# Down projection in a conv FFN: a third pair of output tiles by seven products, with Pool's weight sums held back

## The reference

```python
def conv_ffn(h, w_up, conv_w, conv_b, w_down):
    u = h @ w_up
    c = u.shape[-1]
    u = lax.conv_general_dilated(u, conv_w[:, None, :].astype(u.dtype), window_strides=(1,),
        padding=[(CONV_WIDTH - 1, 0)], dimension_numbers=("NWC", "WIO", "NWC"), feature_group_count=c) + conv_b
    a, gate = jnp.split(u, 2, axis=-1)
    return (jax.nn.silu(gate) * a) @ w_down

x = x + conv_ffn(h, ffn_w_up[layer], ffn_conv_w[layer], ffn_conv_b[layer], ffn_w_down[layer])
```

## Time and profile before

| what | value |
|---|---|
| median of three runs | 3196.84 us (3196.56 to 3198.14) |
| the profiled execution | 3196.49 us |
| its span, first to last instruction | 3194.6 us |
| mean granted TensorE clock | 0.999 |
| PE busy | 3179.1 us, 100% of the span |
| DVE busy | 2049.5 us, 64% |
| ACT busy | 1298.8 us, 41% |
| POOL busy | 503.0 us, 16% |

### The profile page before, as it was taken

One profiled execution on the slowest core, in us unless ns is written; L12 is line 12 of the kernel. 1 busy time (PEld: TensorE's weight loads), 2 busy tenths in 40 slices (PEclk: granted clock), 3 DMA queues, 4 the chain that ended last, 5 costly groups with the idle time before them and its releaser, 6 DMA issues.

```text
span 3194.6 us, 45570 instructions
## 1 busy us (share of the span) xinstructions
PE 3179.1 (100%) x16502; PEld 2681.1 (84%) x16502; DVE 2049.5 (64%) x2876; ACT 1298.8 (41%) x1758; POOL 503.0 (16%) x436
## 2 busy tenths in 40 slices
PE   9999999999999999999999999999999999999998
PEld 7788888889998788888889998768888888888887
DVE  8455567586557455567586555666877744588776
ACT  4433333334443433333334453354443523554433
POOL 2100000123221100000123221052202101322111
PEclk9999999999999999999999999999999999999999
DMA  7256324423333156324423332203233332122332
GB/s 268 67 167 208 125 93 167 142 93 106 100 105 101 58 165 205 130 92 164 146 91 108 99 102 87 86 21 101 97 106 99 105 99 92 47 79 93 105 99 79
DMA packets 100044, 359.31 MB, mean 112 GB/s; under 512 B 11057, under 2 KB 13361, under 8 KB 99761
## 3 DMA queue, kind: packets, MB, share of 16 engines
q1 hardware_dynamic: 98960, 354.08, 33.6%
q0 software_dynamic: 928, 3.17, 0.3%
HBM read 355.11 MB, written 2.10 MB: 112 GB/s over the span
## 4 chain that ended last, share of the span: by engine, by line
PE 94%; DVE 1%; POOLq 1%; issue 1%; ACT 1%; DMA 1%; DVEq 0%; SPq 0%; ACTq 0%; POOL 0%
PE pb L759 21%; PE pb L761 21%; PE pb L760 21%; PE pb L1074 6%; PE pb L1314 3%; PE pb L829 2%; PE pb L831 2%; PE pb L830 2%; PE pb L791 1%; PE pb L792 1%; PE pb L795 1%; PE pb L1182 1%; PE pb L1613 1%; DMA raw<-stream 1%; PE pb L1615 1%
## 5 line engine op out<-in xcount | busy, mean ns | idle before, releaser
L2348 DVE TENSOR_TENSOR lo<-raw,hi 128x1024 fp32r<-128x1024 f32 (+1 forms) x484 | 601.5, 1249 | 320.6 <-ACT hi L1685 294.8
L1685 ACT ACTIVATE hi<-raw 128x1024 fp32r<-128x1024 f32 x484 | 508.5, 1056 | 730.8 <-PE pb L761 436.3
L759 PE MATMUL pb<-yH,hi 128*128 128x512 f32 (+1 forms) x1664 | 644.7, 387 | 0.0
L760 PE MATMUL pb<-yL,hi 128*128 128x512 f32 (+1 forms) x1664 | 644.5, 387 | 0.0
L761 PE MATMUL pb<-yH,lo 128*128 128x512 f32 (+1 forms) x1664 | 644.4, 387 | 0.0
L759 PE MATMUL pb<-hH,hi 128*128 128x512 f32 x1128 | 440.8, 391 | 0.0
L760 PE MATMUL pb<-hL,hi 128*128 128x512 f32 x1128 | 439.3, 389 | 0.0
L761 PE MATMUL pb<-hH,lo 128*128 128x512 f32 x1128 | 439.2, 389 | 0.0
L761 PEld LDWEIGHTS pb<-yH,lo 128*128 128x128 f32 x1664 | 312.6, 188 | 63.7
L760 PEld LDWEIGHTS pb<-yL,hi 128*128 128x128 f32 x1664 | 312.6, 188 | 63.2
L759 PEld LDWEIGHTS pb<-yH,hi 128*128 128x128 f32 x1664 | 312.7, 188 | 63.0
(11 more groups left out here) (537 smaller groups left out, 5550.1 us busy)
## 6 DMA issues: line engine op xcount, KB each, us to landing
raw<-stream SPq DMA_DIRECT2D x648, 512.0 KB, 3.4
yF<-first SPq DMA_DIRECT2D x8, 512.0 KB, 11.9
act<-first SPq DMA_DIRECT2D x8, 512.0 KB, 16.5
x<-xT SPq DMA_DIRECT2D x4, 512.0 KB, 7.0
outT<-act SPq DMA_DIRECT2D x7, 256.0 KB, 2.2
act<-crow POOLq DMA_DIRECT2D x2, 512.0 KB, 5.4
tab<-decay SPq DMA_DIRECT2D x1, 1024.0 KB, 7.7
scr<-ws POOLq DMA_DIRECT2D x2, 256.0 KB, 3.1
```

What stands on the lines that cost most here:

```text
L759: pe.matmul(out, whi, ahi, start=first, stop=False)
L760: pe.matmul(out, whi, alo, start=False, stop=False)
L1685: act.activation(hi[:, s], raw[:, s], ACT.Copy).then_inc(hi_ready, 1)
L2348: dve.tensor_tensor(lo[:, s, 0:width], raw[:, s, 0:width], hi[:, s, 0:width].bitcast(F32), ALU.subtract).then_inc(lo_ready, 1)
```

## The change

Pair two (g = 1) is done by seven products as well, so that `fast_down` on PE keeps two plain tiles in place of four. Its four weight sums are rounded and subtracted one at a time, in the order in which PE wants them (first sum, e2, e4, e3). For all three fast pairs the first sum goes to a buffer of its own instead of over the raw tile; ACT and DVE split only the second half of the pair's second tile, and the first sum separately. PE takes the product with token sum four before the one with the first weight sum. Pool makes t1 of the last token part (DVE did); the fourth token sum's last part is rounded and split ahead of the second and third. Pool starts the weight sums when that fourth one is split (`m_lo` at 6 x slab + 5), where it used to start with `m_last`. SP's load of pair four's tiles now waits for pair two's weight sums, because `DOWN_GROUPS` holds g = 1.

The diff, cut to its core:

```diff
-FAST_DOWN, DOWN_GROUPS = (0, 1), (2, 3)
+FAST_DOWN, DOWN_GROUPS = (0, 1), (1, 2, 3)
...
+                pool.wait_ge(p_full, 5 * (at - 1 if g == 3 else at if g == 1 else at - 2))
+                pool.tensor_tensor(one, a21, a22, ALU.add)
+                pool.drain().then_inc(s1_ready, 1)
+                pool.tensor_tensor(e2, one, a11, ALU.subtract)
...
+                pool.tensor_tensor(e4, a12, e2, ALU.subtract)
...
+                pool.tensor_tensor(e3, a11, a21, ALU.subtract)
+                pool.drain().then_inc(w_sums, 1)
...
-                    pool.wait_ge(m_last, d_slab(layer, j) + 1)
+                    b1, t1 = d_even, d_raw(1, 3)
+                    pool.wait_ge(product, made + KT - 1)
+                    pool.tensor_tensor(t1, b1[:, TH[1]], b1[:, TH[0]], ALU.subtract)
+                    pool.drain().then_inc(m_first, 1)
+                    pool.wait_ge(m_lo, 6 * d_slab(layer, j) + 5)
                     for g in DOWN_GROUPS:
                         down_sums(layer, j, g)
...
-                for group in (range(3), (3,)):
-                    for m in range(KT):
...
+                for m in range(KT):
+                    w = slice((m % 2 * 4 + m // 2) * P, (m % 2 * 4 + m // 2 + 1) * P)
+                    pe.wait_ge(y_ready, y0 + m + 1)
+                    for s in range(2):
+                        ins = three(pb[:, s], hi[:, s, w], lo[:, s, w], midH[:, m], midL[:, m], m == 0, m == KT - 1)
...
-                product_of(other_sum, own(s1, 0), token(1)).then_inc(p_full, 1)
-                product_of(lower_sum, own(s1, 1), token(4)).then_inc(tile_done, 1)
-                pe.wait_ge(e_lo, at + 1)
+                product_of(lower_sum, own(s1, 1), token(4)).then_inc(p_full, 1)
+                pe.wait_ge(e_lo, e_count(layer, j, g) - (3 if g == 1 else 1))
+                product_of(other_sum, own(s1, 0), token(1)).then_inc(tile_done, 1)
+                if g == 1:
+                    pe.wait_ge(m_lo, tokens_made)
+                pe.wait_ge(e_lo, e_count(layer, j, g) - (2 if g == 1 else 0))
                 pe.wait_ge(x_part, added + 1)
                 product_of(one_sum, summed_w(2), token(2), False).then_inc(p_full, 1)
...
+                    if fast:
+                        down_hi(layer, j, 1, 1)
+                        act.wait_ge(m_first, slab + 1)
+                        middle_hi(3, 0, 1)
                     gate(n - 1)
...
                         act.wait_ge(m_last, slab + 1)
-                        middle_hi(3)
-                        tick(0)
+                        middle_hi(3, 3)
+                        middle_hi(3, 1, 3)
+                        down_sum_hi(layer, j, 1)
...
+                elif i == 0:
+                    dve.wait_ge(s1_ready, one_count(layer, j, g) + 2)
...
+                middle_lo(layer, j, 3, 3)
+                down_one_lo(layer, j, 1)
+                middle_lo(layer, j, 3, 1, 3)
+                plain_add(0)
+                one()
+                down_sum_lo(layer, j, 1, 0)
+                plain_add(1)
+                lower()
+                down_sum_lo(layer, j, 1, 2)
+                other()
+                two()
+                down_sum_lo(layer, j, 1, 1)
+                down_lo(layer, j, 2, 0)
+                upper()
+                down_lo(layer, j, 2, 1)
+                last()
                 one, other, two, lower, upper, last = x_adds(layer, j, 2)
+                down_one_lo(layer, j, 2)
+                one()
                 down_sum_lo(layer, j, 2)
-                one()
+                lower()
+                other()
+                two()
                 down_lo(layer, j, 3, 0)
-                other()
-                lower()
-                two()
+                upper()
                 down_lo(layer, j, 3, 1)
-                upper()
                 last()
...
+                    if fast:
+                        down_lo(layer, j, 1, 1)
+                        middle_lo(layer, j, 3, 0, 1)
                     multiplied(n - 1)
```

More of the change, by code:

```diff
@@ L310, in build @@
         d_product = lambda layer, j: layer * (sum(SLABS) - len(SLABS)) + sum(SLABS[:j]) - j
+        d_middle = lambda layer, j: 56 * LAYERS + 8 + layer * (sum(SLABS) + 12) + sum(SLABS[:j])
         gain2 = sb("gain2", [P, 8])
@@ L1281, in fast_down @@
             def fast_down(layer, j, y0):
-                for group in (range(3), (3,)):
-                    for m in range(KT):
[L1285 to L1293, removed]
+                for s in range(2):
+                    pe.wait_ge(lo_ready, tiles.next())
+                    pe.wait_ge(bank_free, banks.next())
+                for m in range(KT):
+                    w = slice((m % 2 * 4 + m // 2) * P, (m % 2 * 4 + m // 2 + 1) * P)
+                    pe.wait_ge(y_ready, y0 + m + 1)
+                    for s in range(2):
+                        ins = three(pb[:, s], hi[:, s, w], lo[:, s, w], midH[:, m], midL[:, m], m == 0, m == KT - 1)
+                        if m == KT - 1:
+                            ins.then_inc(tile_done, 1)
                 for g in DOWN_GROUPS:
@@ L1299, in down_group @@
                 q, at = g % 2, d_at(layer, j, g)
-                tokens_made, added = 4 * (d_slab(layer, j) + 1), 3 * (at - FAST_1)
+                tokens_made, added = 6 * (d_slab(layer, j) + 1), 3 * (at - FAST_1)
                 upper, other_sum, one_sum, lower_sum = (pb[:, b, 0:256] for b in (2 * q, 2 * q + 1, 4 + 2 * q, 5 + 2 * q))
@@ L3014, in other_of @@
                 def other_of():
-                    dve.wait_ge(p_full, p + 2)
+                    dve.wait_ge(tile_done, done.next(2))
                     dve.tensor_tensor(x1[:, TH[1]], Y, x1[:, TH[1]], ALU.add).then_inc(x_part, 1)
@@ L3024, in lower_of @@
                 def lower_of():
-                    dve.wait_ge(tile_done, done.next(2))
+                    dve.wait_ge(p_full, p + 2)
                     dve.tensor_tensor(x1[:, TH[0]], Z, x1[:, TH[0]], ALU.add)
@@ L3047, in fast_down, with plain_add @@
             def fast_down(layer, j):
-                tick(0)
-                middle_lo(layer, j, 3)
-                for k in range(RING):
+                def plain_add(k):
                     drained.next()
@@ L3054, in fast_down @@
                     dve.tensor_tensor(x[:, k], pb[:, k], x[:, k], ALU.add).then_inc(bank_free, 1)
-                    if k in (1, 2):
-                        down_lo(layer, j, 2, k - 1)
+                one, other, two, lower, upper, last = x_adds(layer, j, 1)
+                middle_lo(layer, j, 3, 3)
[14 more added lines that the diff above has]
+                last()
                 one, other, two, lower, upper, last = x_adds(layer, j, 2)
+                down_one_lo(layer, j, 2)
+                one()
                 down_sum_lo(layer, j, 2)
-                one()
+                lower()
+                other()
+                two()
                 down_lo(layer, j, 3, 0)
-                other()
-                lower()
-                two()
+                upper()
                 down_lo(layer, j, 3, 1)
-                upper()
                 last()
@@ L3068, in fast_down @@
                 one()
+                down_one_lo(layer, j, 3)
                 down_sum_lo(layer, j, 3)
+                lower()
                 tick(1)
                 other()
-                lower()
                 two()
@@ L3140, in conv_ffn @@
                         b1, b2 = d_even, A[:, 2]
-                        t1, t2, t3, t4 = (d_raw(i, 3) for i in (1, 2, 3, 4))
-                        dve.tensor_tensor(t1, b1[:, TH[1]], b1[:, TH[0]], ALU.subtract)
+                        t2, t3, t4 = (d_raw(i, 3) for i in (2, 3, 4))
                         dve.tensor_tensor(t3, b2[:, TH[1]], b1[:, TH[1]], ALU.subtract)
```

76 lines of the change are left out of this document (55 added, 21 removed).

## The result

The changed kernel takes 3205.27 us (median of 12 runs, 3204.30 to 3206.22) against 3196.86 for the kernel before (12 runs): a ratio of 1.0026 with a 95% interval of 1.0019 to 1.0034. It is 8.4 us slower. The forecast was 3202.0, 5.2 us slower.

The account below looks back on a forecast made before the run. PE, busy with matmuls without a gap, was taken to bound the kernel. From the profiled 3196.49 us, 3.2 gained and 8.7 of new waits gave +5.5, 3202.0 us; own range 3198 to 3206, full range 3193 to 3210.

Parts of the forecast that it names:

- PE's gain: Pair two on PE: 10.08 us as a fast pair against 10.89 plain, 0.81 us a slab, 3.2 over four slabs.
- The last product: Product m = 7 in the first slab: ready at 8.7 us, asked for at 9.53, so hidden.
- the four places named: PE waits in the down parts at pair two's e2, `other`, pair three's first tile and its sums; 8.7 us in all.
- e2's: Pair two's second weight sum, slab one: split done at 17.85, wanted at 16.65, PE waits 1.26 us; none in slabs two, four.
- The lead of 1.5: In slabs two and four everything comes 1.5 us earlier, which takes e2's wait away: 1.3 us of waits each.
- other: DVE's add in pair two, slab one: done at 19.84, PE wanted it at 19.46, a wait of 0.44 us.
- pair three's first tile: Its split, slab one, stands behind a Pool sum: done at 23.36, wanted at 22.89, a wait of 0.53 us.
- its sums: Pair three's weight sums, slab one: split ends at 29.4, wanted at 29.29, a wait of 0.17 us.
- Slab three: Everything comes 0.4 us later than in slab one: 3.2 us of waits against 2.8.
- Hidden waits: Rival, chance 0.22: the down parts' new waits are hidden; 3193.3 us at the most, 3197.6 with half of the waits.
- Pool as the bound: Rival, chance 0.22: Pool sums behind the first take 2.05 to 2.11 us, 14.3 us of waits; 3207.6 us.
- The clock: Rival, chance 0.02: PE's clock falls to 1.2 GHz after e2's wait in every slab, +5.8 us; 3207.8 us.

Follow-up runs that it names:

- e1: Changed kernel with each of Pool's weight sums in the down part replaced by two memsets, so Pool reads nothing (weight sums left out); 3194.39 us.
- e4: Changed kernel with pair two's four weight sums made earlier by Pool, beside the up tiles, t1 back on DVE, each pair's sums rounded and split together; 3202.79 us.
- e6: Changed kernel with pair two's last three weight sums rounded in one ACT copy and split in one DVE instruction; 3216.80 us.
- e2: Changed kernel with Pool's gate undone: its weight sums start with `m_last`, as in the kernel before; 3201.31 us.
- e5: Changed kernel with pair two's four weight sums made by DVE in place of Pool; 3201.64 us.
- e3: Changed kernel with another order on DVE: the add `other` comes earlier, the second plain add and `lower` later; 3204.85 us.
- e10: Kernel of e5 with DVE's order altered again and Pool starting pair three sooner; 3203.71 us.

## Why the prediction was right, and where it was off

The measured 3205.27 us lies in the forecast's own range of 3198 to 3206, close to its end: the mechanism was right, the loss 1.6 times the one forecast.

- **PE's gain** of 0.81 us a slab was right: e1's undisturbed down parts take 41.11 against 41.91, 0.80 less. (A matmul's spacing exceeds its columns at 2.4 GHz by 13.5 and 13.3 ns in the rows, not by the prediction's 11; the gain does not rest on that.)
- **The last product** was ready at 9.00 after the start (8.7 forecast), before PE asked for it at 9.53: hidden, as said.
- **Places and cause** were right. In the down parts PE waits at the four places named and nowhere else, with Pool's sums of pair two at 1.28 to 1.53 us, and e1, where Pool reads nothing, loses 0.6 in place of 11.4 us.
- **The term that was mis-sized is e2's.** The forecast had e2 split at 17.85 in slab one and a wait of 1.26 that slabs two and four, 1.5 us ahead, would not have. It was split at 18.26: Pool began at 11.57 and not 11.3, its sum for e4 ended at 16.04 and not 15.66, and PE started 0.11 behind the split. So the wait was 1.74: 0.3 of the 0.48 too little is the last product, 9.00 and not 8.7, handed on through the chain, the rest came in at the links behind it. Pool began 1.16 and 1.51 us sooner in slabs two and four, and 1.74 less these leaves 0.58 and 0.23; measured are 0.59 and 0.25. The lead of 1.5 was right in slab four and 0.34 too long in slab two; the wait that it was set against was 0.48 too short. e2 alone is 1.4 of the 2.8 us between the table's 11.5 and the prediction's 8.7.
- **The sum** was added up too low: by the prediction's own terms slabs two and four come to 1.5 each and not 1.3, and with the roundings of the others the four make 9.2 and not 8.7. Its walk thus gives 3202.4.
- **The smaller terms**: other 0.64 (0.56 with its start forecast), pair three's first tile 0.65 (0.65), its sums 0.43 (0.29), in slab one; over the slabs 0.9 us more than forecast.
- **Slab three** was to come 0.4 later than slab one. It took 44.65 us against 44.63: its last product was ready at 9.05, not at 9.5, and Pool began at 11.61.
- **The rivals.** Hidden waits: no. Pool as the bound: by its own point of decision, 2.4 us of waits a slab, it is met on average (2.85 a slab) and by e4's sum in slabs one and three (16.04 and 16.07, limit 15.9; 14.85 and 14.51 in two and four), but its mechanism is not what happened: no sum ahead of e2's split took the 2.05 to 2.11 us of its price; the time lies between the forecast and it. Nothing gained and nothing lost: no, 3.2 us were gained and 11.4 lost. The clock: it stayed at 1.00 in all four down parts, whose longest wait is 1.77, but the longer waits of e4 and e6 did bring it down. The Trainium skill, "TensorE: Matmul & The Clock Gate", section "HAM oscillation — how this bites in real kernels", warns of waits between bursts of matmuls; the trace agrees in e6, behind four waits of 3.1 to 4.7 us, and in e4 behind one of two waits of 2.5.
- **Not foreseen** was that the gate on Pool's sums is itself a loss: without it the kernel is 4.0 us faster (e2). While Pool is held back DVE stands idle: 2.12 us before the first sum's split (row of 2295.14), 0.47 in e2, and in e5, where DVE makes the sums, hardly at all. The prediction took the gate as given, and did not work out the other order.

No version here that makes all the sums is faster than the kernel before. From e4's windows, early sums in slabs two and four alone, with slabs one and three as before, would save 0.17 + 0.51 = 0.7 us of 3197, 0.02%; that was not run.

## What to carry to other kernels

A cheaper form of a product that needs sums of its operands is paid for by the engines that make them: before it is used for one more tile, the vector engines' free time between the last input and the first use must be counted, with each Pool instruction of two SBUF operands entered as time in which DVE can't run a split either. Where that stretch has no idle time, another order only chooses which product waits (e3), or adds to the waits (e10). What helped here is less work in it (e1), a start early enough to use DVE's idle time ahead of it (e2), the sums on DVE, where one takes 0.68 us in place of Pool's 1.3 to 1.5 (e5), and work moved to a stretch that has room (e4 in slabs two and four). And in a walk along such a chain an error at its head, here 0.3 us, comes back at every slab's first wait, also where a lead was thought to cover it.

## What the runs showed of the hardware

- **The clock fell behind the longest waits only, and the same wait did not always bring it down.** In e4 a wait of 2.5 us left the clock at 1.00 in slab one and brought it to 0.50 in slab three, where PE ran at full spacing for some 1.5 us after the wait and then started 15 matmuls of 256 columns 0.21 apart. In e6 waits of 3.1 to 4.7 us brought it to 0.50 in all four slabs, in slab one before the wait had ended, and PE worked at it for some 3 to 5.5 us. Waits of up to 1.77 us in a down part left it at 1.00. e4's times spread over 3200.1 to 3205.8, where most others here keep within about 2 us; that the clock falls in some executions and not in others would explain it, but it was seen in one profile only.
- **A memset on Pool takes no turn with DVE.** Beside memsets of 0.53 us DVE's splits of 512 columns take 0.68 or 0.69 us, as they do alone (e1); beside Pool's sums they take 0.82 to 1.78. The section of the Trainium skill named at e1 says so too: only a GpSimd instruction that reads SBUF counts.
